# Splitting the prompt's attention into groups of 2, 2 and 4 tiles, with two of the eight tiles ahead of the expert stage and a new timetable for the rest

## The reference

```python
z = h @ p['w_in']                                   # q, k, v, gMLP u and v, branch gates
o = attend(q, k, v, lam)                            # per head: softmax map 1 minus lambda * softmax map 2, times v
a_out = rms_norm(o, p['subln_g']) * (1 - lambda_init)
mix = (ga * (a_out @ p['w_att_out']) + gb * (s_out @ p['w_gm_out'])) @ p['w_out']
x = x + g1 * mix
h2 = modulate(x, p['norm2_g'], sh2, sc2)
# PEER, per token and each of 8 heads:
s1, i1 = lax.top_k(s[:, :, 0], 16); s2, i2 = lax.top_k(s[:, :, 1], 16)
top_s, sel = lax.top_k(s1[..., :, None] + s2[..., None, :], 16)   # 16 of 256 candidates
a = einsum('td,thkd->thk', xb, u_tab[idx]); wgt = softmax(top_s) * gelu(a)
y = einsum('thk,thkd->td', wgt, v_tab[idx])
```

## Time and profile before

| | us |
|---|---|
| median of 3 runs (4835.68 to 4861.12) | 4850.87 |
| the profiled execution, its own time | 4868.02 |
| its span, first to last instruction | 4866.2 |
| PE busy | 2975.9 |
| DVE busy | 2538.0 |
| POOL busy | 2711.8 |
| ACT busy | 592.7 |

### The profile page before, as it was taken

How to read it: one execution, slowest core, us unless ns; L and a number is a source line. 1 busy time by engine, 2 the same in 40 slices (tenths; PEclk the granted TensorE clock), 3 DMA queues, 4 the chain that set the end, 5 groups by cost and what they waited for, 6 DMA issues and landing times.

```text
span 4866.2 us, 47305 instructions
## 1 busy us (share of the span) xinstructions
PE 2975.9 (61%) x16593; PEld 1784.3 (37%) x16593; DVE 2538.0 (52%) x5693; ACT 592.7 (12%) x1228; POOL 2711.8 (56%) x2513
## 2 busy tenths in 40 slices
PE   3889999896892667637567737563455323233344
PEld 1666777564781553314343314341122000000000
DVE  2883150332118887864667765556456456456311
ACT  1111241332111013210013310000000000000000
POOL 2222222233223567766677776667667777777675
PEclk7899999877995887768788868786765655655556
DMA  7223221689866999999999999999999999999898
GB/s 285 75 90 134 95 79 60 241 312 359 337 229 236 396 382 398 337 393 418 419 414 400 370 378 406 420 410 373 389 385 390 377 356 364 379 359 358 332 361 302
DMA packets 481519, 1556.44 MB, mean 320 GB/s; under 512 B 52150, under 2 KB 121207, under 8 KB 465884
## 3 DMA queue, kind: packets, MB, share of 16 engines
q0 software_dynamic: 351376, 1271.99, 67.9%
q1 hardware_dynamic: 129068, 269.21, 14.8%
q10 hardware_dynamic: 864, 12.58, 0.6%
HBM read 1488.47 MB, written 65.23 MB: 319 GB/s over the span
## 4 chain that ended last, share of the span: by engine, by line
POOL 33%; DMA 15%; PE 13%; issue 12%; DVE 5%; another core or an unknown queue 2%; POOLq 1%; ACT 0%; SPq 0%; DVEq 0%; ACTq 0%
POOL v_rows L964 17%; POOL u_rows L955 15%; DMA v_rows<-in_peer_v,expertsT 11%; PE ps_y L1288 5%; DVE u_rows L1857 2%; DMA u_rows<-in_peer_u,experts 2%; DMA v_rows<-in_cache_v 2%; PE ps_bank L1142 2%; PE ps_bank L1066 1%; PE ps_bank L1148 1%; PE ps_y L1247 1%; PE ps_bank L1069 1%; PE ps_y L1206 1%; PE ps_bank L1090 0%
## 5 line engine op out<-in xcount | busy, mean ns | idle before, releaser
L1857 DVE CUSTOM_DVE_ANT_0 u_rows<-u_rows,h_rows 128x1024 f32<-128x1024 f32 x1056 | 1290.6, 1224 | 1157.4 <-DMA u_rows<-in_peer_u,experts 831.0
L1288 PE MATMUL ps_y<-v_rows,w_columns 128*32 128x512 f32 x4224 | 865.7, 952 | 1442.3 <-DMA v_rows<-in_peer_v,expertsT 1329.7
L964 POOL DMA_INDIRECT v_rows<-in_peer_v,expertsT x1056 | 1172.7, 1111 | 604.2 <-issue 288.6
L955 POOL DMA_INDIRECT u_rows<-in_peer_u,experts x1024 | 1119.0, 1093 | 454.1 <-issue 295.5
L1288 PEld LDWEIGHTS ps_y<-v_rows,w_columns 128*32 128x32 f32 x4224 | 171.1, 147 | 1995.3 <-issue 1993.8
L365 PE MATMUL ps_z<-w_in_high,hT_high 128*128 128x512 f32 (+1 forms) x1008 | 401.5, 398 | 29.0 <-ACTq L389 26.7
L365 PE MATMUL ps_z<-w_in_high,hT_low 128*128 128x512 f32 (+1 forms) x1008 | 398.3, 395 | 0.0
L365 PE MATMUL ps_z<-w_in_low,hT_high 128*128 128x512 f32 (+1 forms) x1008 | 397.1, 394 | 0.0
L340 POOL CAST w_in_high<-w_in_buf 128x4096 fp32r<-128x4096 f32 x13 | 47.6, 3661 | 491.3 <-PE ps_z L365 460.7
L1148 PE MATMUL ps_bank<-turned_a,weights 128*128 128x256 f32 (+1 forms) x1280 | 271.9, 373 | 4.2 <-issue 3.3
L1142 PE MATMUL ps_bank<-weights,turned_a 128*128 128x256 f32 (+1 forms) x1152 | 267.0, 391 | 5.9 <-issue 4.0
(11 more groups left out here) (241 smaller groups left out, 3576.0 us busy)
## 6 DMA issues: line engine op xcount, KB each, us to landing
u_rows<-in_cache_kT POOLq DMA_DIRECT2D x128, 512.0 KB, 6.1
v_rows<-in_cache_v POOLq DMA_DIRECT2D x128, 512.0 KB, 6.2
weights<-in_peer_w_q SPq DMA_DIRECT2D x40, 1024.0 KB
w_in_buf<-in_w_in POOLq DMA_DIRECT2D x14, 2048.0 KB, 9.1
scratch_z<-z_out SPq DMA_DIRECT2D x112, 256.0 KB, 2.0
weights<-in_w_att_out SPq DMA_DIRECT2D x20, 1024.0 KB
weights<-in_w_gm_out SPq DMA_DIRECT2D x20, 1024.0 KB
weights<-in_w_out SPq DMA_DIRECT2D x20, 1024.0 KB
```

The lines of the kernel that those rows point to most:

```text
L955: pool.indirect_dma_start(ur[:, n % RU, :], None, g.peer_u, bass.IndirectOffsetOnAxis(ap=col, axis=0)).then_inc(s_ur[n % RU], 16)
L964: pool.indirect_dma_start(vr[:, n % RV, :], None, g.peer_v, bass.IndirectOffsetOnAxis(ap=idxT[:, t % 3, k:k + 1], axis=0)).then_inc(s_vr[n ...
L1288: last = nc.tensor.matmul(ps_y[32 * j:32 * (j + 1), b:b + CB], wcol[:, base:base + 32], vr[:, (V0[t] + i + j) % RV, b:b + CB], start=r == ...
L1857: nc.vector.tensor_tensor_reduce(ur[:, n % RU, :], ur[:, n % RU, :], hrow[:, t % 2, :], 1.0, 0.0, ALU.mult, ALU.add, a[:, s:s + 1]).then_i ...
```

## The change

`GROUPS_ATT` becomes (0, 1), (2, 3), (4, 5, 6, 7). The front keeps the attention of tiles 0 and 1 alone (23 steps instead of 39). The expert stage takes four parts, each spread evenly over its ticks: attention 1 with mix 1 (58 steps) over ticks 0 to 51, attention 2 with mix 2 (74 steps) over ticks 52 to 115, mix 3 over 116 to 167, mix 4 over 168 to 231. Where there are more steps than ticks, some ticks hold two steps. Because mix 1 and mix 2 end in tick 19 of tiles 1 and 3, the selections of tiles 2 and 4 (in tiles 1 and 3, `LATE`) move to slots 84 to 124 with two steps a slot, and their score loads to tick 20.

```diff
-GROUPS_ATT = ((0, 1, 2, 3), (4, 5), (6, 7))
+GROUPS_ATT = ((0, 1), (2, 3), (4, 5, 6, 7))
+def timetable(parts):
+
+    ticks, slots = {}, {}
+    for steps, begin, end in parts:
+        for i, step in enumerate(steps):
+            ticks.setdefault(begin + i * (end - begin) // len(steps), []).append(step)
+    for tick, steps in ticks.items():
+        for n in range(TICK * len(steps)):
+            slots.setdefault(TICK * tick + n // len(steps), []).append(steps[n // TICK] + (n % TICK,))
+    return ticks, slots
...
-    S0 = 36
+    S0, S1 = 36, 84
...
-    BACK = every("mix", 1) + every("att", 1) + every("mix", 2) + every("att", 2) + every("mix", 3) + every("mix", 4)
+    BACK = ((every("att", 1) + every("mix", 1), 0, 52),
+            (every("att", 2) + every("mix", 2), 52, 116),
+            (every("mix", 3), 116, 168),
+            (every("mix", 4), 168, 232))
+    LATE = (1, 3)
+    AT_TICK, AT_SLOT = timetable(BACK)
...
-                        if tick == 8:
+                        if tick == (20 if t in LATE else 8):
                             load_scores(t + 1)
...
-                        if t < PT and S0 <= s < S0 + STEPS:
+                        if t < PT and t not in LATE and S0 <= s < S0 + STEPS:
                             select(t + 1, s - S0)
-                        tick = t * TPT + s // TICK
-                        if t < PT and tick < len(BACK):
-                            kind, p, k = BACK[tick]
-                            background[kind](p, k, s % TICK)
+                        if t in LATE and S1 <= s:
+                            for i in range(2 * (s - S1), min(2 * (s - S1) + 2, STEPS)):
+                                select(t + 1, i)
+                        for kind, p, k, quarter in AT_SLOT.get(t * P + s, ()) if t < PT else ():
+                            background[kind](p, k, quarter)
```

More of the change, by code:

```diff
@@ L599, in tail_phase @@
     place, main, last_in = {}, 0, {}
-    for step in FRONT + BACK:
+    for step in FRONT + [step for steps, _, _ in BACK for step in steps]:
         for key in units(*step):
@@ L818, in mix @@
                         if m < PT // 2:
-                            p = max(0, m - 1)
+                            p = next(n for n, tiles in enumerate(GROUPS_ATT) if tl[0] in tiles)
                             for b in range(2):
@@ L925, in _ @@
                     for tick in range(TPT if t < PT else 0):
-                        if t * TPT + tick < len(BACK):
-                            kind, p, k = BACK[t * TPT + tick]
+                        for kind, p, k in AT_TICK.get(t * TPT + tick, ()):
                             background[kind](p, k)
-                        if tick == 2 and 1 <= t < PT:
+                        if tick == (21 if t in LATE else 2) and 1 <= t < PT:
                             sp.wait_ge(s_u, U0[t])
@@ L1296, in _ @@
                     for tick in range(TPT):
-                        if t < PT and t * TPT + tick < len(BACK):
-                            kind, p, k = BACK[t * TPT + tick]
+                        for kind, p, k in AT_TICK.get(t * TPT + tick, ()) if t < PT else ():
                             background[kind](p, k)
@@ L1463, in _ @@
                     for tick in range(TPT):
+                        if t in LATE and tick == 29:
+                            gate_exp(t + 1)
+                        for kind, p, k in AT_TICK.get(t * TPT + tick, ()) if t < PT else ():
+                            background[kind](p, k)
                         if t and tick in (0, 1, 9, 17):
@@ L1467, in _ @@
                                 columns(t - 1, part)
-                        if t < PT and t * TPT + tick < len(BACK):
-                            kind, p, k = BACK[t * TPT + tick]
-                            background[kind](p, k)
                         if t < PT and tick % 4 == 3:
@@ L1474, in _ @@
                             gelu(t, (18, 31).index(tick))
-                        if t < PT and tick == 25:
+                        if t < PT and t not in LATE and tick == 25:
                             gate_exp(t + 1)
```

## The result

The changed kernel took 4869.49 us (median of 17 runs, 4860.26 to 4895.29) against 4841.98 us for the kernel before (17 runs, 4829.75 to 4865.14): a ratio of 1.006, 95% interval 1.0046 to 1.0074. It is 0.6% slower, some 28 us, where +2 us had been forecast. The time lies in the range, just past the 0.5% that was taken as no change. That says little by itself: the range of 125 us also holds all three rivals' times.

What follows compares the result with a forecast made beforehand. No single engine bounds the kernel: PE and DMA are near full in the front, DMA in the expert stages. Front -51, stage 0 +29, stages 1 to 7 +24 make +2 on 4851: 4853 us, range 4795 to 4920.

Steps and rivals of the forecast that it cites:

- The step that failed: Expert stages: moved score loads and other moves counted as hidden; a late score load would cost DVE 5 to 10 us.
- The front: Before stage 0: less attention there wins 51 us, 17 up to sample step 17 and 34 behind; bounds 25 to 89.
- The front hardly shrinks: Rival, front: the samples' pages pace it and only PE's 25 us go; +28 us, 4879 us; chance 0.10.
- Stage 0: First expert stage: attention of tiles 2 and 3 makes DVE set the pace, 286 us against 257, a loss of 29.
- The stretch from slot 84 to slot 84: 128 slots from tile 1 to tile 2: DVE leads with 430 us, 50 above 380; bounds 407 and 456.
- mutual waiting: In the 128 slots from slot 84 of tile 1: engines waiting on each other raise DVE's 407 us to 430.
- The longer gathers: Expert stages: u gathers take 1250 ns beside attention, 1013 in stage 6; POOL might want 439 us in the 128 slots.
- Stages 1 to 7: Expert stages after the first: 2802 us against 2778, a loss of 24, between 1 and 50.
- attention's interplay: Stages 1 and 3: attention costs 21 and 19 us more than their bytes explain, 40 us taken out of the sum.
- DVE's waits double: Rival, stages 0 to 2: a tile-head's waits grow from 0.95 to 1.9 us; +48 us, 4899 us; chance 0.22.
- The expert stage absorbs it: Rival: front wins 80 us with DMA engines full, stage 0 loses only 14; -42 us, 4809 us; chance 0.30.
- rival C: Posed for the follow-up runs, no chance given: packing more steps into the ticks of stages 0 to 3 is the price.

Runs made afterwards that it cites:

- e1: The changed kernel with the score loads of tiles 2 and 4 issued on SP ahead of the tick's other work; ratio to the kernel before 1.0021.
- e4: The changed kernel with the front's attention (tiles 0 to 3) and tile 2's selection as in the kernel before; ratio to before 0.9999.
- e10: e4 without the attention of tiles 2 and 3, and with score loads ahead of the tick's other work; ratio to the kernel before 0.9887.
- e5: e1 without the attention of tiles 2 and 3, whose mix reads the attention rows of tiles 0 and 1; ratio to the kernel before 0.9951.
- e11: e1 with PE adding up v rows ahead of a tick's steps in seven ticks of eight; ratio to the kernel before 1.0164.
- e2: The changed kernel with attention 2 and mix 2 in ticks 63 to 115 instead of 52 to 115; ratio to the kernel before 1.0055.
- e8: The changed kernel with tile 2 selected early, attention 1 and mix 1 in ticks 0 to 39, score loads first, h2 load moved; ratio to before 0.9989.
- e9: e8 with attention in four groups of two tiles, no late selection, and the h2 load moved in stage 3 too; ratio to before 0.9974.

## Why the prediction came out as it did

The form was right: time moved from the front into the expert stages. The sum missed by 26 us, and one step carries most of it. Without that step's stall e1 is 10 us over before by its ratio, near the forecast, but in part by luck: the front and stage 0 came out 17 us better than in the sum (by the means of the profiles), and stages 1 to 7 some 8 us worse.

**The step that failed** is the sentence on the moves that are "hidden by the 11 ticks or the steps that follow", with 5 to 10 us for a late score load, once in each of the two tiles. The load was late in tile 1 alone, by 25.6 us, and undoing that (e1) gave back 0.4%. The sum had it at nothing, and no row was given for its slack. There are no 11 ticks for it: it stands in tick 20, and slot 84 is the first slot of tick 21. What stood ahead of it on SP was not priced: the loads of L789 and L791 took SP 0.38 and 0.58 us at 1971 us and 10.34 us each a few us later. The kernel before showed a late score load of 16.9 us in stage 2, and the prediction doesn't mention it.

**The front** (51 us predicted, bounds 25 to 89): 57 by the mean of two profiles, 54 by e4 and e10. Its division was off. Sample step 17 starts at 1049.8 us with the change against 1087.9 in the earlier trace rows (second profiles: 1045.6 and 1074.2), 33 us earlier on average and not 17, past the bound of 22. The prediction held the DMA work up to there at 178 us; but 359 GB/s for 162 us are 58.2 MB, 6 MB less than the 64.4 MB of the earlier trace rows. At 0.96 x 162 = 156 us the DMA work had shrunk too. This stands in the row:

```profile
888.00:1050.00 162.00, 131.15 (x1426) 87.57 (x1430) 51.55 (x192) 44.65 (x125) 59.62 (x113) 0.77 0.96 359
```

Behind it 24 us were won where 34 were taken. The two errors (16 and 10 us) largely cancel, which is luck. Over 888 to 1398 us the front's DMA share is 0.90, at the edge of the sign that was named. The rival by which the front hardly shrinks is refuted.

**Stage 0** (+29 predicted, 271 to 312 us): +18, 274 us. DVE's work was put at 271 us without waits and is 261; DVE is 0.95 busy, as said, and its waits are mostly hidden. By e5 and e1 the attention itself costs 24 us there (248.2 to 272.4). The DMA share is 0.91 and not at most 0.8; the bytes are as counted (325 GB/s x 275 us = 89 MB, 88 predicted).

**The stretch from slot 84 to slot 84** (430 us, bounds 407 to 456): 454.5 and 449.7, 437.9 in e1 without the stall; in the kernel before it took 410. The size was near and the reason not. DVE was to lead with a share above 0.9, and in e1 it is busy 366 of 438 us, 0.84:

```profile
1999.00:2437.00 438.00, 334.92 (x1610) 176.35 (x1602) 365.86 (x982) 142.92 (x370) 300.50 (x258) 0.82 0.93 348
```

No compute engine is full there, and the DMA share is 0.93. PE is late with the v rows, and POOL waits for buffers. The addition for "mutual waiting" comes nearest to what the table of POOL's waits measures. The longer gathers that the prediction weighed don't show: over stages 1 to 3 the mean u gather holds POOL for 1100 ns with the change and 1130 before. The first double-selection slots stay under 4.3 us (184.4 us for 44 slots with the stall, 4.2; 161.6 in e1, 3.7).

**Stages 1 to 7** (+24 predicted, bounds 1 to 50): +57 by the mean of two profiles; less the stall of 25 us, +32. The late selection of tile 2 holds POOL for 10.0 us and that of tile 4 for none it shows, 10 in all against 6. The 40 us of attention's interplay, which the sum takes out of stages 1 and 3, are a term that the runs don't bear out. Stage 3 has no attention left with the change, and by the same count (399 GB/s x 422 us less 134 are 34 MB) it is still 422 - 367 - 34 = 21 us over its bytes, where before it was 19. In e4, whose stage 3 has no attention either and no tick with two steps, 14 us are left:

```profile
2592.00:3002.00 410.00, 221.87 (x1103) 124.11 (x1101) 233.80 (x535) 31.40 (x57) 284.93 (x257) 0.75 1.00 398
```

So a part of that price isn't attention's; both have tile 4's late selection, but what it is, is not shown. Stages 4 to 7 win 22 us where "within 15" was said, a part of it as in e4. The background costs 1 us a MB as taken: stage 6 now has 380 us x 388 GB/s = 147 MB, 13 over the gathers, and is 13 us longer than in the earlier trace rows. The page "DMA: Bandwidth & Descriptors" of the Trainium skill, section "Issuing engines are not separate DMA queues", says that the time to initiate a DMA is usually small beside the DMA; by the rows of SP above this case differs, since issues of 5.2 to 10.3 us ahead of the scores are what made them late.

**The rivals.** "The front hardly shrinks" had the nearest time, +28 us and 4879, by a mechanism that is refuted: the front won 57 us, not 25. "DVE's waits double" (+48, 4899 us) doesn't show either: in the stretch all rows of DVE's waits inside attention steps come to 41 us, 1.3 a tile-head for 32, and in stage 0 to 1.8 us for 16, so 0.9 on average where the rival had 1.9. "The expert stage absorbs it" had stage 0 about right (+14) and the front too large (80).

**What stays open.** Why PE is late with the v rows. It is not which of rows and steps comes first in a tick (e11), not two selection steps a slot by themselves (e2), and not the work of one engine alone (e5 beside e10). Nor is PE short of time as a whole: over stages 1 to 3 it waits 330 us for v gathers with the change and 369 before. How densely steps stand in the ticks of stages 1 to 3 goes with it (e2 dearer, e8 and e9 cheaper), but density, the engines' waits in attention steps and the late selection weren't varied one by one; the 31 us from e10 to e5 hold all three. So rival C is neither shown nor refuted.

## What to carry to other kernels

A load that something waits for belongs ahead of the bulk loads of its tick on the issuing queue, and its slack is read from the waits and issue times of what stands ahead of it, where the DMA engines are full. Before a deadline is moved, look in the trace for a wait on the same load; one was there. When an engine counts out the stages with a fixed number of issues, split its time into issuing and waiting for buffers in every version: here the waiting carried the difference.

## What the runs showed of the hardware that was not expected

- The same two loads on SP (`qk_rows`) took 0.38 and 0.58 us to issue, and 10.34 us each a few us later; in e1 up to 12.53 us. In the 80 us from 1960 us on, where the long ones lie, SP's queue moved 7648 packets of 0.7 KB on average (5.51 MB), and POOL's 6947 of 3.6 KB, at about 410 GB/s in all until the wait for the scores. What held the issues up, no run shows:

```profile
q0 software_dynamic: 6947, 25.29, 78.4%
q1 hardware_dynamic: 7648, 5.51, 21.3%
```

- Two profiles of the same kernel before differ by 66 us in span (4866.2 and 4800.2), more than twice the effect that was studied; by stages, 17 us of it lie in stage 1 alone. The kernel's median also moved between sets of runs, from 4816.5 to 4842.0 us. One profile a side can't carry a comparison of 0.6%; the ratios with intervals do, and the profiles say where.
